# A two-layer block on one core: normalised rows made anew in a down projection, and the bounded gates' operations in other slots

## What is computed

```python
def _modulate(x, g, shift, scale):
    return _rmsnorm(x, g) * (1 + scale) + shift

def _swiglu(h, w1, w3, w2):
    return (jax.nn.silu(h @ w1) * (h @ w3)) @ w2

def _forget(f_raw, lb):                       # once forward, once backward
    log_f = jnp.logaddexp(jnp.log(lb), jnp.log1p(-lb) + jax.nn.log_sigmoid(f_raw))
    k = (1.0 - lb) * jax.nn.sigmoid(-f_raw)
    return k, log_f

# second layer, after its mixer: latent tokens only
lat = lat + 0.5 * ml[8] * _swiglu(_modulate(lat, norm_ffn2_g[l], ml[6], ml[7]), *ffn2)
```

## Time and profile before

| | us |
|---|---|
| median of three runs | 2616.95 |
| the profiled execution | 2619.17 |
| its span on the core | 2617.4 |

### The profile page before, as it was taken

The page is one execution under the profiler, slowest core; times in us unless marked ns, Lnnn a source line. Parts: engine busy times, 40 slices in busy tenths (PEclk is TensorE's granted clock), DMA queues, the critical chain, the costliest instruction groups (busy, mean ns, idle before and its releaser), DMA issues.

```text
span 2617.4 us, 43989 instructions
## 1 busy us (share of the span) xinstructions
PE 2569.0 (98%) x17111; PEld 2290.2 (87%) x17111; DVE 1222.5 (47%) x1865; ACT 1105.2 (42%) x1538; POOL 889.7 (34%) x1092
## 2 busy tenths in 40 slices
PE   7999999999999999999999999999999999999999
PEld 5777779988897777797777798899999999999999
DVE  4222325227752232252232257675567566656754
ACT  4322333635444122244122247544674554446533
POOL 1222222320022222222222226315554455553554
PEclk9999999999999999999999999999999999999999
DMA  7443543330034334433444433234544444552454
GB/s 282 141 168 140 165 149 117 139 128 1 33 120 146 145 145 145 145 110 132 145 145 145 145 138 133 110 109 180 184 169 165 137 161 177 182 185 100 164 188 147
DMA packets 58528, 376.90 MB, mean 144 GB/s; under 512 B 6223, under 2 KB 12007, under 8 KB 14216
## 3 DMA queue, kind: packets, MB, share of 16 engines
q1 hardware_dynamic: 56988, 371.53, 39.2%
q10 hardware_dynamic: 1388, 3.16, 0.8%
HBM read 370.46 MB, written 3.16 MB: 143 GB/s over the span
## 4 chain that ended last, share of the span: by engine, by line
issue 58%; POOL 22%; PE 17%; DVE 1%; POOLq 1%; DMA 0%; ACT 0%; SPq 0%; DVEq 0%; ACTq 0%
POOL WL L1993 22%; PE PSA L583 5%; PE PSA L585 5%; PE PSA L584 5%; PE PSA L1342 0%; POOLq L405 0%; PE PSA L1240 0%; PE PSA L1267 0%; DMA X<-in_x 0%; DMA RAW<-in_weights 0%; PE PSA L665 0%; POOLq L1991 0%; ACT WH L1412 0%; PE PSA L1258 0%; PE PSA L1228 0%
## 5 line engine op out<-in xcount | busy, mean ns | idle before, releaser
L1993 POOL TENSOR_TENSOR WL<-RAW,WH 128x256 fp32r<-128x256 f32 x1088 | 889.5, 846 | 1715.3 <-ACT WH L1412 1715.3
L1412 ACT ACTIVATE WH<-RAW 128x1024 fp32r<-128x1024 f32 x544 | 545.8, 1050 | 936.6 <-PE PSA L585 918.0
L2016 DVE TENSOR_TENSOR WL<-RAW,WH 128x1024 fp32r<-128x1024 f32 x272 | 339.6, 1249 | 1077.5 <-ACT WH L1412 1077.2
L583 PE MATMUL PSA<-HH,WH 128*128 128x512 f32 (+2 forms) x1664 | 596.3, 358 | 9.4 <-DVE WL L2016 3.4
L584 PE MATMUL PSA<-HL,WH 128*128 128x512 f32 (+2 forms) x1664 | 588.6, 354 | 0.0
L585 PE MATMUL PSA<-HH,WL 128*128 128x512 f32 (+2 forms) x1664 | 588.0, 353 | 0.0
L583 PE MATMUL PSA<-GH,WH 128*128 128x256 f32 (+1 forms) x1664 | 527.0, 317 | 6.8 <-DVE GL L2033 5.7
L584 PE MATMUL PSA<-GL,WH 128*128 128x256 f32 (+1 forms) x1664 | 521.0, 313 | 0.0
L585 PE MATMUL PSA<-GH,WL 128*128 128x256 f32 (+1 forms) x1664 | 520.8, 313 | 0.0
L583 PEld LDWEIGHTS PSA<-HH,WH 128*128 128x128 f32 x1664 | 315.7, 190 | 69.0 <-issue 17.6
L585 PEld LDWEIGHTS PSA<-HH,WL 128*128 128x128 f32 x1664 | 315.8, 190 | 43.2
(11 more groups left out here) (336 smaller groups left out, 2966.1 us busy)
## 6 DMA issues: line engine op xcount, KB each, us to landing
RAW<-in_weights SPq DMA_DIRECT2D x272, 1024.0 KB, 4.8
ADA<-in_w_ada SPq DMA_DIRECT2D x65, 1024.0 KB, 4.9
Zada<-in_w_ada SPq DMA_DIRECT2D x7, 1024.0 KB, 14.5
scratch_bias<-BREL ACTq DMA_DIRECT2D x1, 2048.0 KB
SUMS<-in_c_sums SPq DMA_DIRECT2D x1, 1664.0 KB, 8.7
TB<-scratch_bias SPq DMA_DIRECT2D x1, 1536.0 KB, 11.8
X<-in_x SPq DMA_DIRECT2D x1, 1024.0 KB, 6.8
X<-in_ctx SPq DMA_DIRECT2D x1, 1024.0 KB, 9.3
```

The lines of the kernel that those rows point to most:

```text
L583: pe.matmul(out, a_hi, b_hi, start=start, stop=False)
L1412: act.activation(WH[:, j, 4 * h:4 * h + 4, :], RAW[:, j, 4 * h:4 * h + 4, :], ACT.Copy)\
L1993: ins = pool.tensor_tensor(WL[:, j, kb, :], RAW[:, j, kb, :], WH[:, j, kb, :].bitcast(F32), ALU.subtract)
L2016: dve.tensor_tensor(WL[:, j, 0:4, :], RAW[:, j, 0:4, :], WH[:, j, 0:4, :].bitcast(F32), ALU.subtract)\
```

## The change

Three edits. First, in `pair_by_stream` the call `part_sums(3, 0)` stands ahead of `block(0, 1, 7)` in place of behind it. Second, the first down projection (slots 146 to 149) makes the normalised rows, 1/rms and shift in them: per slot two scaled rows T2 on DVE, two high parts on ACT and two low parts on DVE, between the low part of the weights and the addition to X; the PE waits for all eight of them before slot 150, and the up projections 150 to 155 and 160 to 167 take the unshifted code. The loop over that down projection is written out. Third, in w_in of the second layer log(1 + exp(-|a - b|)) takes the place of log(1 + exp(min - max)): for each direction DVE makes one subtraction fewer and no minimum, ACT one absolute value more, and the operations stand at i = 2, 3, 4 and i = 5, 6, 7.

```diff
--- before.py
+++ after.py
@@ -73,6 +73,7 @@
         plan.append(dict(kind="norm", index=norm, slot=slot, unit=unit, ada=ada, **more))
         norm += 1
     def ffn(l, which, rate, tokens):
+        at = len(plan)
         if l + which == 2:
             plan.append(dict(kind="late_norm", gain="g_ffn2", layer=l, final=False, mods=(6, 7), ada=ada))
         else:
@@ -83,14 +84,16 @@
                 plan.append(dict(kind="decays", part=2 * t - 1))
             if l + which == 0 and t:
                 plan.append(dict(kind=("", "setup_loads", "setup")[t]))
-            phase("ffn_up", nb, nb, rate, tokens=tokens, blocks=nb, layer=l, third=t, shifted=(l + which == 2))
+            phase("ffn_up", nb, nb, rate, tokens=tokens, blocks=nb, layer=l, third=t, shifted=(l + which == 2 and t == 0),
+                  renewed=(l + which == 2 and t == 1))
             if l + which == 0 and t == 2:
                 plan.append(dict(kind="bounds"))
             if t == 0:
                 plan.append(dict(kind="gate", layer=l, mod=2 + 6 * which, half=True, ada=ada))
             if l + which == 2:
                 plan.append(dict(kind="decays", part=2 * t))
-            phase("down", 4, 4, rate, tokens=tokens, kin=nb, gate=2 + 6 * which, layer=l, per=1, first=(t == 0))
+            phase("down", 4, 4, rate, tokens=tokens, kin=nb, gate=2 + 6 * which, layer=l, per=1, first=(t == 0),
+                  renews=plan[at] if l + which == 2 and t == 0 else None)
     for l in range(2):
         both, lat = 512, (512 if l == 0 else 256)
         ffn(l, 0, 1, both)
@@ -739,6 +742,8 @@
                 kind, N = ph["kind"], ph["tokens"] + (2 if ph.get("shifted") else 0)
                 hbase = n.at(h_ready)
                 loop = kind not in ("w_in", "in_even", "in_odd")
+                if ph.get("renewed"):
+                    n.take(h_ready, KB)
                 def h_block(kb):
                     pe.wait_ge(h_ready, hbase + kb + 1)
@@ -827,8 +832,9 @@
                             pe.wait_ge(bank_read[1], ph["unit"] + BANK_CREDIT)
                         if kb >= ahead:
                             block(1, 1, kb - ahead)
+                        if kb == KB - 1:
+                            part_sums(3, 0)
                         block(0, 1, kb)
-                    part_sums(3, 0)
                     for kb in range(KB - ahead, KB):
                         block(1, 1, kb)
                     for j in range(2):
@@ -1652,6 +1658,12 @@
                 def body(it):
                     for s in range(2 * ph["per"]):
                         after_slot(ph, it, s, 2 * ph["per"])
+                        if ph.get("renews"):
+                            for m in range(2):
+                                n.take(t_ready)
+                                kb = 4 * it + 2 * s + m
+                                act.activation(HH[:, kb, 0:N], T2[:, m, 0:N], ACT.Identity,
+                                               bias=MODS[:, ph["renews"]["mods"][0], kb, 0:1]).then_inc(hh_ready, 1)
                         if ph["squares"] and s % ph["per"] == ph["per"] - 1:
                             v = s // ph["per"]
                             act.wait_ge(bank_read[v], it * 2 + (ph["unit"] + 2 + BANK_CREDIT))
@@ -1664,7 +1676,7 @@
                                     .then_inc(sq_ready, 1)
                 if ph["ends_by_stream"]:
                     return body(0)
-                repeat(act, 2, body, ph is not PLAN[-1])
+                repeat(act, 2, body, ph is not PLAN[-1] and not ph.get("renews"))
                 if ph["squares"]:
                     n.squares += KB
@@ -1864,7 +1876,8 @@
                     act.activation(KK[:, d], KK[:, d], ACT.Exp).then_inc(act_to_dve, 1)
                 if i in (3, 7) and l == 1:
                     n.take(dve_to_act)
-                    link(act.activation(T8[:], T8[:], ACT.Exp))
+                    link(act.activation(T8[:], T8[:], ACT.Abs))
+                    link(act.activation(T8[:], T8[:], ACT.Exp, scale=-1.0))
                     act.activation(T8[:], T8[:], ACT.Ln, bias=1.0).then_inc(act_to_dve, 1)
                 if i == 8:
                     vs = VS[:, 0:4 * (N // P)]
@@ -2421,6 +2434,19 @@
                         after_slot(ph, it, per * v + per - 1, 2 * per)
                 n.skip(h_ready, KB)
+            def renewed_rows(late, k0, N):
+
+                shift, scale = late["mods"]
+                for m in range(2):
+                    if k0:
+                        dve.wait_ge(h_ready, n.at(h_ready) + k0 + m - 1)
+                    dve.scalar_tensor_tensor(T2[:, m, 0:N], X[:, k0 + m, 0:N], MODS[:, scale, k0 + m, 0:1], RSTD[:, 0:N],
+                                             ALU.mult, ALU.mult).then_inc(t_ready, 1)
+                for m in range(2):
+                    n.take(hh_ready)
+                    dve.scalar_tensor_tensor(HL[:, k0 + m, 0:N], T2[:, m, 0:N], MODS[:, shift, k0 + m, 0:1],
+                                             HH[:, k0 + m, 0:N].bitcast(F32), ALU.add, ALU.subtract).then_inc(h_ready, 1)
+
             def down(ph):
                 if ph["feeds"]:
@@ -2432,6 +2458,8 @@
                             after_slot(ph, it, per * v + s, 2 * per)
                         if v and ph["ends_by_stream"]:
                             add_unit(True, slice(0, N))
+                        if ph.get("renews"):
+                            renewed_rows(ph["renews"], 4 * it + 2 * v, N)
                         dve.wait_ge(mm_done, it * (2 * per) + (ph["slot"] + per * v + per))
                         for m in range(2):
                             for s, t in streams(N):
@@ -2445,7 +2473,9 @@
                             ins.then_inc(bank_read[v], 1)
                 if ph["ends_by_stream"]:
                     return body(0)
-                repeat(dve, 2, body, ph is not PLAN[-1])
+                repeat(dve, 2, body, ph is not PLAN[-1] and not ph.get("renews"))
+                if ph.get("renews"):
+                    n.skip(h_ready, KB)
                 if ph["rate"]:
                     rows_copy(ph)
@@ -2737,6 +2767,10 @@
                 l, N = ph["layer"], ph["tokens"]
                 tbs = N // P
+                if i == 4 and l == 1:
+                    n.take(act_to_dve)
+                    link(dve.tensor_tensor(LF[0][:], LF[0][:], T8[:], ALU.add))
+                    dve.engine_nop().then_inc(decay_ready, 1)
                 if i in (1, 4):
                     d = (1, 4).index(i)
                     n.take(act_to_dve)
@@ -2744,22 +2778,21 @@
                     dve.tensor_tensor(KK[:, d], LF[d][:], KK[:, d], ALU.subtract).then_inc(dve_to_act, 1)
                 if i in (2, 5) and l == 1:
                     d = (2, 5).index(i)
-                    lf = LF[d][:]
                     dve.wait_ge(lb_landed, 48)
-                    link(dve.tensor_tensor(lf, lf, bc(LBT[:, 1, d, :], 4), ALU.add))
-                    link(dve.tensor_tensor(T8[:], lf, bc(LBT[:, 0, d, :], 4), ALU.min))
-                if i in (2, 6) and l == 1:
-                    d = (2, 6).index(i)
-                    lf = LF[d][:]
-                    link(dve.tensor_tensor(lf, lf, bc(LBT[:, 0, d, :], 4), ALU.max))
-                    dve.tensor_tensor(T8[:], T8[:], lf, ALU.subtract).then_inc(dve_to_act, 1)
-                if i in (3, 7):
-                    d = (3, 7).index(i)
+                    link(dve.tensor_tensor(LF[d][:], LF[d][:], bc(LBT[:, 1, d, :], 4), ALU.add))
+                    n.take(act_to_dve)
+                    link(dve.tensor_tensor(KK[:, d], KK[:, d], bc(LBK[:, d, :], 4), ALU.mult))
+                if i in (3, 6) and l == 1:
+                    d = (3, 6).index(i)
+                    link(dve.tensor_tensor(T8[:], LF[d][:], bc(LBT[:, 0, d, :], 4), ALU.subtract))
+                    dve.tensor_tensor(LF[d][:], LF[d][:], bc(LBT[:, 0, d, :], 4), ALU.max).then_inc(dve_to_act, 1)
+                if i == 3 and l == 0:
+                    n.take(act_to_dve)
+                    dve.engine_nop().then_inc(decay_ready, 1)
+                if i == 7:
                     n.take(act_to_dve)
                     if l == 1:
-                        link(dve.tensor_tensor(KK[:, d], KK[:, d], bc(LBK[:, d, :], 4), ALU.mult))
-                        n.take(act_to_dve)
-                        link(dve.tensor_tensor(LF[d][:], LF[d][:], T8[:], ALU.add))
+                        link(dve.tensor_tensor(LF[1][:], LF[1][:], T8[:], ALU.add))
                     dve.engine_nop().then_inc(decay_ready, 1)
                 if i == 8:
```

## The result

| | before | after | ratio, 95% |
|---|---|---|---|
| median, six runs each | 2617.16 us | 2626.99 us (2621.45 to 2629.57) | 1.0033 [1.0024, 1.0043] |
| profiled execution (its span) | 2619.17 (2617.4) | 2621.45 (2619.7) | |

The change costs about 9 us: a third of a per cent, clearly more than the measurement leaves open. 2619.2 had been forecast, and at most 2625. One thing has to be kept in mind for all that follows: the profiled execution of after is the quickest of its six. Its trace shows each pause, but it is lucky in its clock: the second profile of the same kernel (e4) took 2627.29 us, with 6.8 us more at the lower clock.

A forecast was written before the change was run, and what follows sets the result against it. The PE, busy 2569.0 of 2617.4 us, was taken as the bound. Terms -2.9 + 2.0 + 3.2 = +2.3 us on the 2616.95 us median gave 2619.2 us, range 2611.7 to 2625.

The forecast's parts named there:

- Part 1: Latent rows, four places: the sum starts one block, 0.72 us, earlier; -2.9 us, bounds -2.0 and -3.6.
- Part 2: w_in of the second layer: ACT's longer chain delays slots 127 and 130; +2.0 us, bounds -1 and +4.
- Its last step: w_in, direction 1: ACT's chain frees the bank at 1643.2, so slot 130 starts then, not at 1641.3.
- Rival A: w_in: shorter DVE work lets POOL finish in time, pauses and low clock go; -6.6 there, 2610.7 us in all; chance 0.15.
- Part 3: Rows made anew, down projections and slot 150: gains at later slots against new pauses; +3.2 us, from 0 to +6.
- pause at slot 156 (3.07) and in 168 (1.57): Later down projections: unshifted code shortens the chain to `GL`, pauses fall to 1.3 and 0.1 us; together -3.2 us.
- low clock behind slot 156: The stretch of 3.5 us at the lower clock behind slot 156 goes with the shorter pause: -1.5 us.
- pause ahead of slot 150: Slot 150 waits for all eight new rows, ready about 5.5 us behind slot 149: +5.4 us, bounds 3.6 and 6.1.
- low clock behind it: Behind the pause at slot 150, 3.4 us at the lower clock: +1.5 us, bounds 0 and +3.0.
- slot 148, additions behind the rows: Slot 146's bank is free 6.3 us behind its end, slot 148 wants it at 5.8: +0.5 us (0 to 1.1).
- slots 158 and 160: Small pauses there, DVE's `decays` no longer covered by the pause at 156: up to 0.5 us more.
- rival B's first condition: 7 us at 1.2 GHz follow slot 150's pause (+1.5); the rival, clock down longer, gave 2622.9 us, chance 0.27.

The follow-up runs named there:

- e4: The changed kernel, all three edits, run again unchanged beside the kernel before: 2626.96 us, ratio 1.0031; its profile took 2627.29 us.
- C: The first edit, the sum moved (`part_sums(3, 0)` ahead of `block(0, 1, 7)`); alone against the kernel before: 2614.46 us, ratio 0.9981.
- e2: Only the w_in edit (new formula, operations placed anew) against the kernel before: 2621.07 us, ratio 1.0010.
- e5: The moved sum and the w_in edit together, without the new rows, against the kernel before: 2618.88 us, ratio 1.0004.
- e7: The changed kernel, but slot 150 waits for each row with its first block, not for all eight: 2621.06 us, 1.0009 against the kernel before.
- e9: The moved sum, and the new w_in formula with its operations in the old places, against the kernel before: 2615.96 us, ratio 0.9990.
- e1: Only the sum moved, against the kernel before: 2614.46 us, ratio 0.9981.
- e8: The moved sum and the new rows, each pair made one slot earlier, without the w_in edit, against the kernel before: 2610.97 us, ratio 0.9976.
- e12: Only the sum moved against the kernel before, run once again for a second profile: 2613.53 us.
- e6: The moved sum and the new rows together, without the w_in edit, against the kernel before: 2620.67 us, ratio 1.0009.
- W: The third edit, w_in's new formula with its operations placed anew; alone against the kernel before: 2621.07 us, ratio 1.0010.
- B: The second edit, the rows made anew in the first down projection; alone against the kernel before: 2624.26 us, ratio 1.0022.
- e3: Only the rows made anew in the first down projection, against the kernel before: 2624.26 us, ratio 1.0022.

## Why the prediction was wrong

**Part 1** was right in mechanism and size: the chain from the sum on moved by 0.72 us in all four places, nothing else became late, and L2168 fell to 1.1 us as forecast. What was not seen is that C alone also keeps w_in and slot 156 at the full clock.

**Part 2** was right in its size and in its first steps. ACT's weights of slot 126 are 3.4 us late, slot 127 pauses 2.3 us (2.1 forecast), the half of slot 128 pauses 3.1 as before. Its last step, that slot 130 starts when ACT lets it, holds in e2 (a wait of 1.8 us) and in e4, e5 and e7 (0.3 to 0.4), but not in the trace of after: there ACT has emptied the bank by 1636.47, and slot 130 begins without a wait at 1637.4. What is lost there is lost in the pauses, with a new one of 0.9 us at slot 128 that had not been forecast: 6.3 us in place of 4.4, the lower clock lasting 6.8 us in both. +2.0 us forecast; +3.0 by e2's runs, and +2.1 in the trace of after (131.62 - 130.21, and 0.72 of the sum), so that in this trace the number was met in part by luck. Rival A, the relief of POOL, fell as argued, by its own condition: the low part of slot 127 was not done in time. e9 shows that its mechanism is real in the old places, and that ACT's longer chain takes it away there too.

**Part 3 is the step that failed**, with +3.2 us forecast where the trace has +6.4 us (148 to 158: 7.2; 158 to 170: -0.7; 136 to 148: -0.1). Term by term:

| term | forecast | after |
|---|---|---|
| pause at slot 156 (3.07) and in 168 (1.57) | -3.2 | -3.4 (1.26 is left, and nothing) |
| low clock behind slot 156 | -1.5 | -1.5 |
| pause ahead of slot 150 | +5.4 | +6.3 |
| low clock behind it | +1.5 | +2.4 |
| slot 148, additions behind the rows | +0.5 | +1.3 |
| slots 158 and 160 | +0.5 | +0.8 (slot 160: 1.28, 0.46 before) |

The terms add up to +5.9, the stretches to +6.4. The 1.5 us for the low clock behind slot 156 are a gain against before only: e1 has it without any new rows.

The pause of 6.3 us is 0.2 from the last matmul to ACT's start, 1.1 to the low part, 1.1 for it, 3.5 for the four operations (0.88 each from start to start, 0.85 had been estimated) and 0.3 until the PE starts. The prediction had the middle three, whose terms give 5.65 where 5.5 was written, and left out both ends. At slot 148 the same slip stands: its four terms make 6.55, not 6.3. And the clock is low for 6.8 us, not 3.4: rival B's first condition, which had been named for just this pause. The Trainium skill ("SBUF — State Buffer", section "Who interferes with whom") bears out the size of the four operations: DVE instructions with two SBUF inputs contend with POOL's reads. The trace agrees: at slot 150 each of the four took 0.94 us while POOL made its half of the weights. In e8 POOL ended at 1824.24, and of the two low parts of rows the one begun before took 0.96 us, the one begun after 0.47.

**The sum over the parts.** These steps give -2.9 + 2.1 + 6.4 = +5.6 us, where +2.3 was forecast; the runs have +8 to +9. The rest, about 3 us, is a term that the prediction put at nothing: the clock in places that the change does not touch, so far as it is seen. Where e4's trace is longer than before's outside these places is in the two mixers (slots 48 to 50: 129.87 against 128.27 us; 134 to 136: 83.60 against 81.84), each by 3.4 us more at the lower level. The profile of after happens to have neither (126.63 and 81.79). These are 5.1 of the 5.8 us between the two profiles of this kernel, and it is by this luck that the first met the forecast of 2621.5 for a profile. The prediction took the clock as a price of single pauses; it also varies in places that the change does not touch, between two profiles of one kernel (slots 48 to 50: none in after and 6.8 us in e4, 6.8 in e1 and 3.4 in e12), and the profile of one run does not show that.

**What stays open:** why the same pauses bring the lower clock in one kernel and not in another. In w_in the kernels with C and the old formula escape it in all four profiles, and those without C, or with the new formula, do not; behind slot 156 all with C escape it. In the mixer of the second layer five profiles have 10.2 us of it (e2, e4, e5, e6, e7) and the others 6.8. Four of these five have W; of the five profiles with W only after lacks it, though it is the same kernel as e4, and of the nine others e6 alone has it. That hints at W, and no run shows why. Whether W and B meet was not run without C.

## What to carry to other kernels

Ahead of a phase that needs rows from the phase before it, ask which engine step still starts only with the end of the last slot: work placed behind that step is a pause in full, and moving the same work one slot earlier turned +2.5 us into -6.6 us here. An operation taken from a busy engine gains nothing where the replacement lengthens the chain of another that frees a bank; follow both chains to the first matmul that needs them. Where equal pauses of the PE are followed by the lower clock in one profile and not in the next, forecast from several profiles, and give the clock a range of its own.

## What the runs showed of the hardware

The lower clock did not follow the length of a pause in a simple way. Two pauses of 1.50 and 3.09 us, 8.8 us apart, were followed by 0 (four profiles), 3.4 (one) or 6.8 us (two) at 1.2 GHz; one of 3.19 us at slot 156 by 0 (four), 3.4 (two) or 6.8 us (one). A pause of 6.3 us was followed by 6.8 us in each of four profiles (after, e3, e4, e6), and pauses of 1.3 to 1.7 us between slots 136 and 170 by none. In e2 pauses of 2.45 and 2.05 us in w_in were each followed by 3.4 us, and one of 3.09 us between them by none. "TensorE: Matmul & The Clock Gate" of the Trainium skill, section "HAM oscillation — how this bites in real kernels", says that waits between bursts bring the low clock back; the runs agree, but a single trace does not tell whether a given wait will. The kernel before itself spread from 2615 to 2621 us over 84 runs; the three with a mean granted clock of 0.997 took 2615.5 us on average, the six with 0.994 took 2619.9.
